# Seven late modulation pages inside attention, through two weight slots, and expert 2's pages loaded before the output projection

## The reference, cut to what matters

```python
mod = (cond @ p['w_ada'][i] + p['b_ada'][i])[:, None, :]
sh1, sc1, g1, sh2, sc2, g2 = jnp.split(mod, 6, axis=-1)
h = rmsnorm(x, p['g_norm1'][i]) * (1 + sc1) + sh1
m = even_mixer(...) if i % 2 == 0 else odd_mixer(...)   # layer 0: conv + differential attention
x = x + g1 * m
h = rmsnorm(x, p['g_norm2'][i]) * (1 + sc2) + sh2
x = x + g2 * hmoe(h, ...)       # 32 experts, two per token, hidden width 512
```

## Time and profile before

| What | Value |
|---|---|
| Median of three runs | 1759.44 us (1757.55 to 1762.16) |
| The profiled execution: its time, its span | 1752.78 us, 1750.9 us |
| TensorE matmul busy in the span | 1535.3 us (88%) |
| VectorE, ScalarE, GpSimd busy | 611.3, 253.1, 254.9 us |
| Mean granted TensorE clock | 0.977 |
| Moved by the transfer engines | 534.23 MB, 305 GB/s on the mean |
| First layer's attention loop | about 278 to 366 us |
| Output projection, then routing, of the first layer | to 453, to 485 us |
| Experts of the first layer | 485 to 959 us |
| Experts of the second layer | 1246 to 1717 us |

### The profile page before, as it was taken

One profiled execution on the slowest core, in us unless ns is written; L12 is line 12 of the kernel. 1 busy time (PEld: TensorE's weight loads), 2 busy tenths in 40 slices (PEclk: granted clock), 3 DMA queues, 4 the chain that ended last, 5 costly groups with the idle time before them and its releaser, 6 DMA issues.

```text
span 1750.9 us, 19846 instructions
## 1 busy us (share of the span) xinstructions
PE 1535.3 (88%) x6774; PEld 706.6 (40%) x6774; DVE 611.3 (35%) x1186; ACT 253.1 (14%) x505; POOL 254.9 (15%) x391
## 2 busy tenths in 40 slices
PE   4999898989889999989897599999999999898881
PEld 2445444545433333333232355545433333333330
DVE  2399635743612222212121430334522222122215
ACT  3110024631110000000000310012000000000002
POOL 0024020000112121212111200000121211111110
PEclk9999999999999999999999799999999999999996
DMA  9745253380889999999997810254899999999995
GB/s 351 263 172 188 97 192 108 116 306 36 343 336 419 419 419 420 420 420 420 420 419 320 320 49 12 102 223 161 313 420 419 418 418 420 420 420 420 419 420 226
DMA packets 119112, 534.23 MB, mean 305 GB/s; under 512 B 18617, under 2 KB 19442, under 8 KB 68610
## 3 DMA queue, kind: packets, MB, share of 16 engines
q1 hardware_dynamic: 95984, 493.43, 70.0%
q0 software_dynamic: 12544, 21.21, 3.3%
q10 hardware_dynamic: 10514, 18.63, 3.0%
HBM read 522.60 MB, written 27.36 MB: 314 GB/s over the span
## 4 chain that ended last, share of the span: by engine, by line
PE 38%; SPq 18%; DMA 15%; DVE 3%; issue 3%; ACT 2%; ACTq 0%; POOLq 0%; DVEq 0%
SPq L509 18%; PE psum_pair_B L1881 13%; DMA scratch<-w_up 8%; PE psum_pair_C L1903 7%; PE psum_pair_A L1758 4%; PE psum_pair_B L1758 4%; DMA weight_ring<-w_up 3%; PE psum_pair_C L1805 3%; PE psum_pair_D L1805 3%; DMA scratch<-modulation_rows 1%; PE psum_pair_D L1890 1%; DMA scratch<-expert_rows 1%; DVE scratch L1429 1%; PE psum_pair_D L1798 1%; ACT scratch L965 1%
## 5 line engine op out<-in xcount | busy, mean ns | idle before, releaser
L1881 PE MATMUL psum_pair_B<-weight_ring,gates_by_token 128*64 128x512 f32 x1408 | 315.5, 597 | 25.0 <-DMA weight_ring<-w_up 21.4
L1429 DVE TENSOR_TENSOR scratch<-psum_pair_B,scratch 128x256 f32<-128x256 f32 x72 | 30.6, 425 | 513.1 <-ACT scratch L965 513.1
L1881 PE MATMUL psum_pair_B<-scratch,gates_by_token 128*64 128x512 f32 x896 | 199.3, 593 | 10.4 <-DMA scratch<-w_up 10.4
L1881 PEld LDWEIGHTS psum_pair_B<-weight_ring,gates_by_token 128*64 128x64 f32 x1408 | 112.9, 138 | 220.1 <-issue 196.5
L1903 PE MATMUL psum_pair_C<-weight_ring,scratch 128*64 128x512 f32 x704 | 160.8, 597 | 25.0 <-issue 22.6
L756 POOL DMA_INDIRECT expert_rows<-scratch,scatter_rows x72 | 73.6, 1023 | 717.5 <-DVE scratch L1441 717.5
L965 ACT ACTIVATE scratch<-psum_pair_B 128x256 f32<-128x256 f32 x72 | 27.7, 384 | 842.1 <-PE psum_pair_B L1881 842.1
L1758 PE MATMUL psum_pair_A<-scratch,weight_ring 128*128 128x128 f32 (+1 forms) x512 | 144.6, 441 | 4.8 <-DVE scratch L1480 2.8
L1758 PE MATMUL psum_pair_B<-scratch,weight_ring 128*128 128x128 f32 (+1 forms) x512 | 141.9, 435 | 0.0
L1881 PEld LDWEIGHTS psum_pair_B<-scratch,gates_by_token 128*64 128x64 f32 x896 | 74.8, 137 | 130.1 <-issue 119.0
L1523 DVE SCALAR_TENSOR_TENSOR weight_ring<-weight_ring,params 128x655 f32<-128x655 f32 x120 | 117.0, 975 | 4.9
(11 more groups left out here) (382 smaller groups left out, 1437.9 us busy)
## 6 DMA issues: line engine op xcount, KB each, us to landing
weight_ring<-w_gate SPq DMA_DIRECT2D x88, 1024.0 KB, 27.3
weight_ring<-w_up SPq DMA_DIRECT2D x88, 1024.0 KB, 28.1
weight_ring<-w_down SPq DMA_DIRECT2D x88, 1024.0 KB, 28.1
weight_ring<-w_ada SPq DMA_DIRECT2D x22, 2048.0 KB, 8.9
scratch<-w_up SPq DMA_DIRECT2D x40, 1024.0 KB, 27.8
scratch<-w_down SPq DMA_DIRECT2D x40, 1024.0 KB, 27.6
scratch<-w_gate SPq DMA_DIRECT2D x40, 1024.0 KB, 26.5
weight_ring<-w_in_e SPq DMA_DIRECT2D x5, 2048.0 KB, 12.8
```

Source lines behind the costliest of these rows:

```text
L1881: ins = mm(PB[B_][CAP * q:CAP * (q + 1), 512 * par:512 * par + 512].rearrange("p (u n) -> p u n", u=2), XGT[par][:, at:at + CAP], w[:, :, ...
```

## The change

Seven late pages run inside the attention loop, one for every three units, through slots 1 and 0 in turn. Page 7 alone is left in the routing, in slot 4; GpSimd stores its row and waits for all eight stores ahead of the row values instead of behind them, and ScalarE copies its sums ahead of the two exponentials. Expert 0's gate and up pages are loaded when pages 5 and 6 have been multiplied. Expert 2's up and down pages (slots 7 and 8) are loaded at the end of attention, where pages 6 and 7 were. Fillers take the place of the products that left the routing.

```diff
-                  (1, ada(1, 4)), (1, ada(1, 5)), (1, ada(1, 6)), (1, ada(1, 7)), (1, ada(1, 8)),
-                  (4, ada(1, 9)), (7, ada(1, 10)), (8, ada(1, 11))],
+                  (1, ada(1, 4)), (0, ada(1, 5)), (1, ada(1, 6)), (0, ada(1, 7)), (1, ada(1, 8)), (0, ada(1, 9)), (1, ada(1, 10)),
+                  (4, ada(1, 11))],
...
-        IN_ATTENTION = 5
+        IN_ATTENTION = 7
...
                 if l == 0:
-                    late_page(0)
+                    for m in range(IN_ATTENTION):
+                        late_page(m)
                     page_free(sp, owners[0])
                     load(0, 0, 0)
-                    for m in range(1, IN_ATTENTION):
-                        late_page(m)
                     page_free(sp, owners[1])
                     load(0, 0, 1)
                     sp.wait_ge(sig("cat_u"), HC)
                     for i in range(2):
                         sp.wait_ge(sig("raw_stored", i), 16 * ((IN_ATTENTION + 1 - i) // 2))
-                    late_page(5)
+                    late_page(7)
                     page_free(sp, ("av", NU - 1))
                     sp.wait_ge(sig("outputs_stored"), 32)
-                    late_page(6)
-                    late_page(7)
+                    load(2, 2, 1)
+                    load(2, 2, 2)
...
                 if l == 0:
-                    for m, st, kind in ((5, 1, 1), (6, 2, 1), (7, 2, 2)):
-                        page_free(sp, LATE[m])
-                        load(st, st, kind)
+                    page_free(sp, LATE[7])
+                    load(1, 1, 1)
                 page_free(sp, ("weights", l))
                 load(2, 2, 0)
...
                 if l == 0:
                     late_out(0)
                     scaled_router(0)
-                    late_out(5)
-                    late_out(6)
+                    late_out(7)
+                    for i in range(2):
+                        pool.wait_ge(sig("raw_stored", i), 16 * 4)
...
                 pool.tensor_tensor(VAL[:, 1], EQ, rows_flat[1].unsqueeze(2).broadcast_to([128, 10, NBLK]), ALU.mult).then_inc(sig("row_values"), 1)
-                if l == 0:
-                    late_out(7)
-                    for i in range(2):
-                        pool.wait_ge(sig("raw_stored", i), 16 * 4)
...
                 stored(NT - 1)
+                if l == 0:
+                    late_rows(7)
                 act.wait_ge(sig("router_z"), 2 * l + 1)
...
                 if l == 0:
-                    late_rows(5)
-                    late_rows(6)
-                    late_row(5)
-                    late_rows(7)
-                    late_row(6)
                     late_row(7)
...
-                m, part = (i - 1) // 4, (i - 1) % 4
+                m, part = i // 3, i % 3
...
                 if l == 0:
-                    late_products(5)
-                    late_products(6, (0,))
-                    keep_busy(2)
+                    late_products(7)
+                    keep_busy(3)
...
                 if l == 0:
-                    late_products(6, (1,))
-                    late_pick(5)
-                    late_products(7)
-                    late_pick(6)
-                    keep_busy(2)
                     late_pick(7)
-                    keep_busy(4)
+                    keep_busy(9)
```

More of the change, by code:

```diff
@@ L278, in build @@
         LATE = [("ada", 1, c) for c in range(4, 12)]
-        IN_ATTENTION = 5
+        IN_ATTENTION = 7
         LATE_ORDER = [(what, m) for m in range(IN_ATTENTION) for what in ("products", "pick")]
-        LATE_ORDER += [("products", 5), ("products", 6), ("pick", 5), ("products", 7), ("pick", 6), ("pick", 7)]
+        LATE_ORDER += [("products", 7), ("pick", 7)]
         LATE_COUNT = {step: n + 1 for n, step in enumerate(LATE_ORDER)}
@@ L1703, in late_products @@
                         pe.wait_ge(sig("late_taken"), LATE_COUNT[("pick", m - 1)])
-                    elif m >= IN_ATTENTION + 2:
-                        pe.wait_ge(sig("late_taken"), LATE_COUNT[("pick", m - 2)])
                 for k in range(4 * halves[0], 4 * halves[-1] + 4):
```

## The result

The changed kernel takes 1747.38 us on the median of four runs (1745.22 to 1748.47), against 1759.60 for the kernel before, run beside it: a ratio of 0.9929, with a 95% interval of 0.9908 to 0.9950. That is 8.8 to 16 us less, 12.2 by the medians; I had forecast 8.7. The profiled executions lie closer together: 1747.2 us (span 1745.4) after, against 1752.78 (span 1750.9). In later runs an execution here and there took 2389 to 7091 us; all medians and ratios leave these out.

A forecast was written before the change was run, and what follows sets the result against it. The first refill of expert 0's page was taken to bound the kernel. An 8.7 us earlier refill, plus 0 for attention, took the 1759.44 us median to 1750.7, range 1746.5 to 1757.

The forecast's parts named there:

- What bounds the kernel: Experts: SP's first refill of an expert 0 page sets the end; 458.6 and 457.7 us follow it in the two layers.
- Part 1: First layer's routing: pages 5 and 6 leave, page 7's store moves ahead; table 1.35 us earlier, gather issued 3.04 us earlier.
- the template: The second layer's routing, without late pages, its times less 767.01 us taken for the changed first layer.
- Part 2: First block's gather: expert 2's up and down pages loaded at the end of attention shorten it by 3.27 us.
- my first rival: Gather stays slow because expert 2's gate page is loaded beside it: only 3.0 us of issue saved, 1756.4 us; chance 0.12.
- the objection: In the second layer the gate page's load follows 2.6 us behind the gather, and would in the first layer too.
- Part 3: First block on TensorE: rows land 6.31 us earlier, products take 7.10 us for 9.11, first refill 8.7 us earlier.
- Part 4: Attention takes two more pages: net cost 0, bounds a gain of 1.5 and a loss of 6.3 us.
- The sum: Whole kernel: 8.7 us gained plus 0 for attention, 1759.44 to 1750.7 us.

The follow-up runs named there:

- the late store: Changed kernel with page 7's store and the wait for all stores put back behind the row values: 1750.55 us, ratio 0.9944 to the kernel before.
- the backlog run: Changed kernel with expert 2's up and down pages issued in the routing again, behind expert 1's up page: 1754.18 us, ratio 0.9959 to the kernel before.
- second profile: Changed kernel run once more, nothing altered: 1752.32 us, ratio 0.9930 to the kernel before.
- the run with the gate page beside it: Changed kernel with the first layer's first gather also waiting for the row-weight products, so it goes out beside expert 2's gate page: 1760.48 us, ratio 1.0007.
- its twin with fillers: The backlog run plus two more TensorE fillers behind the first layer's row-weight products: 1752.77 us, ratio 0.9958 to the kernel before.
- the run with fillers: Changed kernel with fillers in three idle places of TensorE, in the table and the second layer's routing: 1747.01 us, ratio 0.9919 to the kernel before.

## Why the prediction was right, and where its reason was wrong

**What bounds the kernel** held: what the profiles show as won came through the first refill, and 458.5 to 458.8 us follow it (459.45 where the gate page is late in the kernel before).

**Part 1** held in size. The table ends 18.75 us after the router product instead of 20.09 (1.34; predicted 1.35), the gather is issued 3.01 us earlier (3.04). The store's issue came 2.4 us later than my estimate, at 463.01 for 460.6, well ahead of the row values. That the store stands ahead of them was not needed, as the late store showed. ScalarE's copy ahead of the exponentials cost nothing: TensorE's table is where the template put it.

**Part 2 is the step that failed in its reason.** "I take all of it, because the pages issued ahead of it then match": the size is about right (3.3 to 3.5 us to the turned rows, 3.9 to their landing; predicted 3.27), but the pages ahead were not what made the gather slow before. The gate page was: put back beside the gather it makes it 6.84 us long without any backlog, and taken away from the kernel before it leaves 2.91 with the end of the backlog still in flight. That is the mechanism of my first rival, which expected it to stay; it went because the gather came out 2.5 us ahead of the gate page (475.00 against 477.53), the objection that I had set against that rival. The early load of up and down is still needed, though: with the gather 3 us earlier the old backlog would not have drained, and costs 2.0 us of gather (6.08 for 4.07 to the turned rows; 6.0 for 3.6 to their landing) and 2.8 of clock (9.92 for 7.09), as the backlog run shows.

The gather of the second block, which GpSimd issues next, says the same in all fourteen profiles and both layers, with no clock in it. In the changed kernel it goes out 0.2 us ahead of the gate page (477.34, 477.53); in that kernel's second profile the page comes 1.25 us behind it (479.07, 480.32). From issue to landing, in us, first the one and then the other:

```profile
gates_by_token<-h_rows,row_index_table POOLq DMA_INDIRECT x1, 7.3
...
gates_by_token<-h_rows,row_index_table POOLq DMA_INDIRECT x1, 2.7
```

Wherever the page follows by 0.2 us this gather takes 7.2 to 8.2 us, and wherever it follows by 1.25 us or more, 2.7 to 3.2. It is not on the chain: even the slow one of the changed kernel lands at 484.6, ahead of the end of block 0's products.

So what counts in these runs is whether the transfer engines are full while the gather is in flight, whoever filled them: over the flight of the first block's gather they are 1.01 busy in the backlog run, 0.89 in the run with the gate page beside it, and 0.24 in the changed kernel. How much is queued is another matter, as transfers of the changed kernel show (issues, KB each, median us to landing):

```profile
weight_ring<-w_gate SPq DMA_DIRECT2D x88, 1024.0 KB, 27.2
...
gates_by_token<-h_rows,gather_rows POOLq DMA_INDIRECT x68, 6.7
```

Among the experts SP's pages take 27.2 us to land, the gathers beside them 6.7. So these gathers did not stand behind all that SP had queued. In the routing of the fourteen profiles the gathers of the first two blocks took 5.6 to 8.2 us where the engines were 0.79 to 1.01 busy over their flight, and 2.7 to 4.3 where they were 0.11 to 0.66 busy; neither they nor those among the experts are held for the queue's 27. The routing alone could not tell: in the backlog run the rows landed within 0.3 us of the last page in flight, and so they did beside the gate page. How the engines share their time between the queues no run shows.

**Part 3** held. The products take 7.09 us for 9.09, at a granted clock of 1.00 throughout (480.48 to 487.58), where the kernel before had 0.56 over 485 to 490; the backlog run and its twin with fillers (9.92, 7.09) show that this is the clock, lost in the wait. Refill: 9.04 and 7.94 us earlier in two profiles, 9.05 with fillers; predicted 8.7. The 7.94 has the clock falling behind the table of that execution, which the prediction did not foresee.

**Part 4** held at its value of nothing: 174.42 and 175.28 us against 174.99 twice. The units keep 4.41 us. The wait for page 4 is gone, and the first gap's filling gave 1 us (unit 1: 286.19 to 290.79, 4.60 us, against 5.56), though not in every execution: in the run with fillers that unit took 5.57 again (288.99 to 294.56). One thing was sized too small. VectorE's wait for the shift and scale rows, the kernel before and then the changed kernel:

```profile
386.61 1.23 DVE L1234 TENSOR_TENSOR gates_by_token<-x_residual,scratch 128x1024 f32<-128x1024 f32 x1 [1.78 <-DMA scratch<-modulation_rows]
...
393.82 1.23 DVE L1226 TENSOR_TENSOR gates_by_token<-x_residual,scratch 128x1024 f32<-128x1024 f32 x1 [6.78 <-DMA scratch<-modulation_rows]
...
399.98 0.69 DVE L1212 TENSOR_TENSOR weight_ring<-psum_pair_D,gates_by_token 128x512 f32<-128x512 f32 x1 [2.09 <-PE psum_pair_D L1795]
```

It is 6.78 us instead of 1.78, so 5 later and not 2; the wait for TensorE one tile on shrank from 6.41 to 2.09, and nothing reached TensorE. 2.1 us of cover are left.

**The sum**: 8.7 forecast; 12.2 by the medians of the first measurement, 8.8 to 16 by its interval, and 7.6 by the medians of the second. The forecast stands just outside that interval and between the two medians. Routing accounts for 8 to 9 of it. What the first medians have above that stays open: the profiles vary by up to 5.6 us ahead of the first score (277.9 to 283.5), by up to 6 between the last landing of the first layer's experts and the second layer's last router product (268.9 to 274.8 us; 270.1 to 273.9 in the kernel before), and by 2.4 in its routing.

## What to carry to other kernels

A short transfer on which a chain waits is judged by what fills the transfer engines while it flies: what is still in flight from before, and what another queue issues right beside it. Here a 2 MB page 0.9 us behind a gather was as bad (7.55 us) as one 0.9 us ahead (6.84), and one 1.25 us behind did no harm (2.7); order the big page behind it, or the small one ahead. Two stages of one kernel that differ in the wait are a good template for its size and a poor one for its cause: several things differ at once, and one added wait in the old kernel parted them. Where the work behind a wait is TensorE's, count the clock with the wait, and cover gaps: in the backlog run the clock took 2.74 us and the idle time was 1.85.

## What was not expected

- TensorE's granted clock fell behind gaps no longer than 1.06 us, among fillers and small matmuls (0.50 in 1230 to 1235, with TensorE busy for all of it), in some executions of one kernel and not in others; it cost 2.4 us in the second layer's routing and 1.1 to 1.3 in the first's.
- With work taken away a stage was slower, in the one execution that was profiled: nearly all products of two pages left out, 2.9 to 4.4 us more, with the clock at 0.61 to 0.70.
- One page of 2 MB, issued 0.9 us ahead, made a gather 6.84 us long, as against 2.91 where it came later; one that follows 2.5 us behind was not waited for at all.
